# Regrouping plain matmuls between the steps of a chunked recurrence on one Trainium2 core

## The reference

```
state = state * w_t + (state a_t) b_t^T + v_t k_t^T      # per head, 64 x 64
y_t   = state r_t
g     = sigmoid(xg @ g1) @ g2;   v = xv @ w_v            # plain matmuls beside it
out   = (groupnorm(y) + bonus) * g @ w_o
```

## Time and profile before

| what | value |
|---|---|
| median of 3 runs | 2473.57 us (2472.69 to 2474.89) |
| the profiled execution's own time | 2473.13 us |
| its span, first to last instruction | 2471.3 us |
| PE busy in the span | 2442.3 us (99%) |
| DVE / ACT / POOL busy | 1407.0 / 1073.0 / 129.6 us |
| granted TensorE clock, mean | 0.998 of full |

### The profile page before, as it was taken

How to read it: one execution, slowest core, us unless ns; L and a number is a source line. 1 busy time by engine, 2 the same in 40 slices (tenths; PEclk the granted TensorE clock), 3 DMA queues, 4 the chain that set the end, 5 groups by cost and what they waited for, 6 DMA issues and landing times.

```text
span 2471.3 us, 39453 instructions
## 1 busy us (share of the span) xinstructions
PE 2442.3 (99%) x15550; PEld 2003.7 (81%) x15550; DVE 1407.0 (57%) x1743; ACT 1073.0 (43%) x1348; POOL 129.6 (5%) x172
## 2 busy tenths in 40 slices
PE   8999999999999999999999999999999999999997
PEld 6888788877888888888887888888788888888886
DVE  7788566676744454454446644666745445444445
ACT  4455355444444444443334444453544444444332
POOL 2000235420000000000000000000000000000000
PEclk9999999999999999999999999999999999999999
DMA  6556411255666666666656665455566666666554
GB/s 235 188 192 209 128 42 40 69 210 190 193 192 188 187 193 188 187 187 195 192 193 204 198 195 188 147 176 179 180 187 193 188 187 190 187 201 212 194 194 140
DMA packets 225884, 440.88 MB, mean 178 GB/s; under 512 B 13616, under 2 KB 24240, under 8 KB 224672
## 3 DMA queue, kind: packets, MB, share of 16 engines
q1 hardware_dynamic: 221760, 417.38, 54.4%
q0 software_dynamic: 3600, 21.55, 2.6%
q10 hardware_dynamic: 400, 0.18, 0.0%
HBM read 436.96 MB, written 2.10 MB: 178 GB/s over the span
## 4 chain that ended last, share of the span: by engine, by line
PE 97%; DVE 1%; ACT 1%; DMA 1%; issue 0%; POOL 0%; DVEq 0%; SPq 0%; POOLq 0%
PE ps L601 26%; PE ps L603 26%; PE ps L602 26%; PE ps L914 3%; PE ps L1099 1%; PE ps L797 1%; PE ps L1127 1%; PE ps L807 1%; PE ps L630 1%; PE ps L628 1%; PE ps L629 1%; PE ps L858 1%; PE ps L904 1%; PE ps L762 1%; PE ps L941 1%; PE ps L1213 1%
## 5 line engine op out<-in xcount | busy, mean ns | idle before, releaser
L1270 ACT CAST whi<-raw 128x1024 fp32r<-128x1024 f32 x735 | 772.8, 1052 | 1143.7 <-PE ps L603 1087.2
L1713 DVE TENSOR_TENSOR wlo<-raw,whi 128x1024 fp32r<-128x1024 f32 x549 | 669.8, 1224 | 613.1 <-ACT whi L1270 611.1
L601 PE MATMUL ps<-whi,ahi 128*128 128x512 f32 x2172 | 852.0, 392 | 0.0
L603 PE MATMUL ps<-whi,alo 128*128 128x512 f32 x2172 | 846.3, 390 | 0.0
L602 PE MATMUL ps<-wlo,ahi 128*128 128x512 f32 x2172 | 845.7, 389 | 0.0
L603 PEld LDWEIGHTS ps<-whi,alo 128*128 128x128 f32 x2172 | 407.9, 188 | 85.3
L602 PEld LDWEIGHTS ps<-wlo,ahi 128*128 128x128 f32 x2172 | 408.1, 188 | 84.3 <-issue 1.0
L601 PEld LDWEIGHTS ps<-whi,ahi 128*128 128x128 f32 x2172 | 408.0, 188 | 83.6 <-DVE alo L2100 0.7
L2045 DVE TENSOR_TENSOR wlo<-raw,whi 128x1024 fp32r<-128x1024 f32 x193 | 236.1, 1224 | 249.8 <-ACT whi L1270 247.8
L601 PE MATMUL ps<-whi,hThi 128*128 128x512 f32 x656 | 255.6, 390 | 0.0
L603 PE MATMUL ps<-whi,hTlo 128*128 128x512 f32 x656 | 255.4, 389 | 0.0
(11 more groups left out here) (317 smaller groups left out, 1941.8 us busy)
## 6 DMA issues: line engine op xcount, KB each, us to landing
raw<-w_up SPq DMA_DIRECT2D x176, 512.0 KB, 3.6
raw<-w_down SPq DMA_DIRECT2D x176, 512.0 KB, 4.0
raw<-w_gate SPq DMA_DIRECT2D x170, 512.0 KB, 3.6
raw<-w_k SPq DMA_DIRECT2D x32, 512.0 KB, 3.8
raw<-w_r SPq DMA_DIRECT2D x32, 512.0 KB, 4.4
raw<-w_v SPq DMA_DIRECT2D x32, 512.0 KB, 3.9
raw<-w_o SPq DMA_DIRECT2D x32, 512.0 KB, 5.1
raw<-kv_v SPq DMA_DIRECT2D x32, 512.0 KB, 3.7
```

Of the source, the lines that this page charges most:

```text
L601: mm(o, hi[:, k, tok], whi[:, s, k2, :], start=(k == 0), stop=False)
L603: last = mm(o, lo[:, k, tok], whi[:, s, k2, :], start=False, stop=(k == kt - 1))
L1270: nc.scalar.copy(whi[:, s], src).then_inc(hi_done, 1)
L1713: V.tensor_tensor(wlo[:, s], src, whi[:, s].bitcast(F32), ALU.subtract).then_inc(split_done, 1)
```

## The change

`FILL` is rewritten. The number of units in each slot stays what it was; where they stand changes:

| slot | before | after |
|---|---|---|
| 0 | nine places | 3 units of `inner5` stand at `inner4` |
| 1, 3, 4 | state1 2, inner3 1, outer3 2, outer4 2, inner5 3, outer5 4 | state1 2, outer3 2, inner4 6, outer5 4 |
| 2 | as after | unchanged |
| 5 | inner5 3 | inner4 3 |
| 6 | inner1, outer1, inner2 2 each | none there, inner4 6 |
| 7 | outer1, inner2 2 each, outer4 2, inner5 2 | none at the first two, outer4 4, inner5 4 |

The place `inner4` comes right after `transposes_of`. Where it has units and another group follows, ACT does `turned` for both lanes ahead of `outer` 4; before, the second lane's came after it. In slot 7 ACT's `keep_gate` 4 to 6 are each one place later in its order. No instruction is added or taken away.

```diff
-SOME = {"state1": 2, "inner3": 1, "outer3": 2, "outer4": 2, "inner5": 3, "outer5": 4}
+SOME = {"state1": 2, "outer3": 2, "inner4": 6, "outer5": 4}
 FILL = (
-    {"inner1": 3, "outer1": 2, "inner2": 2, "state1": 3, "inner3": 2, "outer3": 3, "outer4": 2, "inner5": 3, "outer5": 4},
+    {"inner1": 3, "outer1": 2, "inner2": 2, "state1": 3, "inner3": 2, "outer3": 3, "inner4": 3, "outer4": 2, "outer5": 4},
     SOME,
     {"state1": 1, "inner3": 1, "outer3": 2, "outer4": 2, "inner5": 4, "outer5": 4},
     SOME,
     SOME,
-    {"state1": 2, "inner3": 2, "outer3": 3, "outer4": 2, "inner5": 3, "outer5": 4},
-    {"inner1": 2, "outer1": 2, "inner2": 2, "state1": 4, "inner3": 2, "outer3": 4, "outer4": 4, "outer5": 4},
-    {"inner1": 4, "outer1": 2, "inner2": 2, "state1": 2, "inner3": 2, "outer3": 2, "inner4": 2, "outer4": 2, "inner5": 2},
+    {"state1": 2, "inner3": 2, "outer3": 3, "inner4": 3, "outer4": 2, "outer5": 4},
+    {"state1": 4, "inner3": 2, "outer3": 4, "inner4": 6, "outer4": 4, "outer5": 4},
+    {"inner1": 4, "state1": 2, "inner3": 2, "outer3": 2, "inner4": 2, "outer4": 4, "inner5": 4},
 )
@@ ACT, in the slot @@
+                outer(s, 2)
                 if s == 7:
                     keep_gate(4)
-                outer(s, 2)
-                if s == 7:
-                    keep_gate(5)
                 if s in (0, 5):
                     keep({0: 4, 5: 6}[s])
                 outer(s, 3)
                 if s:
                     outputs(s - 1)
                 if s == 7:
-                    keep_gate(6)
+                    keep_gate(5)
+                beside = FILL[s].get("inner4", 0) > 0
                 if more:
-                    turned(s + 1, 0)
+                    for a in range(2 if beside else 1):
+                        turned(s + 1, a)
                 outer(s, 4)
                 if s == 7:
+                    keep_gate(6)
                     for g, bank in ((0, 4), (1, 6), (2, 5)):
                         keep_zt(g, bank)
                 if s in (2, 6):
                     keep({2: 5, 6: 7}[s])
-                if more:
+                if more and not beside:
                     turned(s + 1, 1)
```

## The result

| | median us | runs |
|---|---|---|
| before | 2473.57 | 11 (2471.99 to 2475.72) |
| after | 2478.86 | 11 (2477.10 to 2480.22) |

The ratio is 1.0023 (95% interval 1.0015 to 1.0030): 5.3 us slower, where 5.5 was forecast. The profiled execution took 2479.14 us against 2473.13.

A forecast was written before the change was run, and what follows sets the result against it. PE was taken as the bound, busy 217.77 of 224.00 us. Slot terms of +4.7 us and +0.8 for stalls gave +5.5 on the median 2473.57, so 2479.1 us; range 2474.7 to 2482.0.

The forecast's parts named there:

- The sum: All slots: +4.7 us from units, places and waits, +0.8 for stalls, together +5.5 us slower.
- The place at 0.31 and the unit at 0.43: PE: a unit costs 0.43 us, a place 0.31 beyond its units; 16 places go, 5.0 us less PE work.
- Outer 4 to outer 5: Slots 3 and 4: PE waits some 1.5 us for DVE's norm and masking; 4.76 us instead of 5.60, saving 0.84.
- Inner 3 to outer 3: Slots 1, 3, 4: without its unit and place PE gains only 0.10 us and waits 0.6 for the mask.
- Costed at nothing: ACT's earlier copies for lane 1 and later `w_o` loads were both taken as hidden, adding 0 us.
- ACT's order: Lane 1 copies before ACT's work on outer 4 are covered by units; uncovered, outer 4's halves come up to 1.1 us later.
- The `w_o` loads: Behind slot 7: asked for about 3 us later, used some 15 us on; up to 3 us if cover failed.
- The forecast's own signs: Profile after: PE busy about 5 us less, stated waits before outer 5 and outer 3, slot 6's front 3 us shorter.
- The front of slot 6: Slot 6 before its later joins: without three places it shrinks from 11.89 to 8.79 us, -3.10.
- The term for stalls: Fronts of slots 6 and 7 without units: PE idle that nothing released, 0.4 us each, +0.8.
- Slot 7's front: Slot 7 loses two places of 1.17 us, but ACT's hand-over limits outer 2 to 482.4 instead of 484.33: -1.90.

The follow-up runs named there:

- the first experiment: The changed kernel with ACT's copies for the second lane put back behind its work on outer 4 in every slot: 2480.01 us, +6.4 against the kernel before.

## Why the prediction was right

**The sum.** +5.5 was forecast, +5.3 measured. Run by run: slots 1, 3 and 4 4.1 us (forecast 4.0), slots 6 and 7 together 0.4 on their own, with stalls (forecast +0.1). Slots 0 and 5 are left with what remains of the 5.3, 0.8 us (forecast 1.4); in the timelines they have +0.68 and +0.14, the latter with 0.34 of stall less. Each of these differences has an interval of some 2 us either way. That the sum came within 0.2 us is partly luck; the joins below are what was forecast closely.

**The place at 0.31 and the unit at 0.43.** Confirmed: six units at inner4 lengthen inner 4 to outer 4 from 2.52 to 5.11 in slots 1, 3 and 4, 2.59 as summed. With a place and its two units gone, outer 4 to the products of lane 0 takes 0.51 instead of 1.69 in slot 3, and inner 1 to outer 1 takes 3.34 instead of 4.52 in slot 6: 1.18 less each, 1.17 by the sum. The Trainium skill, TensorEngine Tiling (Array Packing), Key Properties, says that changing the tiling mode drains the engine. These rows agree as far as a place costs PE about 0.3 us beyond its units; that draining makes it was not tried apart.

**Outer 4 to outer 5.** 4.75 and 4.76 in slots 3 and 4 against a forecast of 4.76. Slot 1 3.71 against 3.83, slots 0 and 5 4.94 and 4.99 against 5.00, slot 6 5.86 against 5.85. The idle times before outer 5 are 1.51 twice, 0.47 in slot 1 and 0.81 to 0.86 in slots 0, 5 and 6 (forecast 1.5, 0.6 and 0.9). That it is DVE's chain is shown from three sides: lengthening it by 0.60 lengthens the wait by 0.60, taking the norm out of it in slots 3 and 4 wins 2 us, and filling the wait with units costs nothing.

**Inner 3 to outer 3.** 1.66 instead of 1.76, with a wait of 0.46 (forecast 0.6): the 0.10 as forecast. It was read in the timelines, not tried by itself.

**Costed at nothing.** ACT's order: shown, by the first experiment. The `w_o` loads were asked for 8.6 us later than before, not 3: slot 7 itself began 4.95 later, which the 3 left out.
```profile
493.46 3.12 SPq L424 DMA_DIRECT2D raw<-w_o  x4
```
No wait of PE for them appears after slot 7; PE's waits from 276 to 560 name DVE, ACT and issue alone. The half us behind slot 7 is a wait of the first matmul with `w_o` for DVE, 0.9 instead of 0.4; in four runs that leave slot 7's table as it was it is 0.5 to 1.0, so it isn't shown to be the change's. One wait that was costed at nothing did come, though not in the changed kernel's own profile: in five of the eight experiments with slot 7's new table a unit waits 0.27 to 0.36 us for ACT's copy of a gate (L904, released by L1438).

**The forecast's own signs.** Two of them did not come as written. PE was to be busy about 5 us less and was 2.1 less. The 5.0 were summed from start to start, and busy time is not: a matmul that nothing follows counts to its end, where before the next one started earlier and lay over it. In slot 3 the products of lane 1 last 1.05 us, and the next start comes 0.92 behind theirs where nothing waits; the new waits before inner 5 and outer 3 have such ends too. Three places save 0.93 in slot 3, and PE was busy 24.51 us in it instead of 24.90. That these ends make the difference is a reading and was not tried. The front of slot 6 was to shrink by 3 us, or the forecast was wrong; it shrank by 1.88, from 11.89 to 10.01 (448.11 to 458.12). In it stands a stall:
```profile
456.58 0.27 PE L858 MATMUL ps<-a2t 64*64 64x64 f32 x2 [1.02 <-issue]
```
Inner 2 to outer 2 takes 2.92 there and 1.67 in slot 3, where no stall stands between the two: 1.25 more. Without that the front is 8.76, and 8.79 was summed. So the step held and the stall, a term of its own in the sum, hid it.

**What was off.** The term for stalls was +0.8 in slots 6 and 7; they came to 1.02 and 0.30. Slot 7's front won 1.3 and not 1.9: outer 2 came as early as summed (487.30 against 484.33 in a slot that began 4.95 later), but from there to the first state unit it took 1.87 instead of 1.20, of which 0.30 shows as idle. That it was too small went unnoticed in the sum because slots 1 to 5 had fewer stalls in this execution. Those vary between executions of the same order on PE: 4.1 us in slots 1 to 5 in the one of before, 2.8 in the one with the extra Newton step, whose PE program is the same. What starts them stays open. They lie in dense runs of small matmuls. Slot 6 had one in every profile in which its front was without units, and none in the others; slot 7 had one in three of nine profiles with its new table. In slots 1 to 5 a unit between brought them from 2.8 to 4.1 us down to 1.0, in one profile.

The run with the norm behind the mask of inner 5 and, in part, the one with a unit in the front missed for one reason: I looked for the next wait at outer 5 alone. DVE's chain goes on to the next inner 1, and the units behind outer 5 cover only its second half. The run with the norm around the mask of inner 4 in all slots missed for another, the delayed short operations ahead of that mask. Why the Newton step in the changed kernel cost 3 us more than its timeline shows is open.

## What to carry to other kernels

A filler that costs 0.3 us in changes of mode can still be worth its place: compare it not with zero but with the longest in-order chain of the other engines that runs beside it, from where they get their input to where PE needs their output. With that chain written down from the timeline (here 4.75 us in slots 3 and 4 against 2.9 of PE's own work, 0.52 + 0.92 + 0.52 + 0.92 from start to start), the number of units that belong inside it follows, and only the rest should be put where they cost no change of mode. After moving something off such a chain, read the next join too, since moving it within the chain only moves the wait.

## What the runs showed of the hardware

Short DVE operations on 8 elements a partition took 1.19 and 1.26 us instead of 0.17 when they began within 0.1 us behind the start of a GpSimd operation of 1.27 us, and ended 0.02 us behind it; in the changed kernel's slot 7 one takes 1.26 as well, and one that began 0.64 us into such an operation takes 0.67. The Trainium skill, SBUF — State Buffer, Who interferes with whom, says that only the port pair that DVE and GpSimd share causes contention and that it is an exclusive lock; these rows agree with a DVE operation that can't end before GpSimd's does. I had summed DVE's small operations at their undisturbed length, and in the two kernels with the norm moved in all slots that cost a wait of 1.39 us in slot 7.

PE stalls of 0.15 to 1.5 us with no semaphore behind them, in runs of 64x64 matmuls without a wider one between, were in every profile, in different slots and sizes.
